# The experts' down weights, issued by ScalarE instead of the sync engine

## What is computed

```python
# t: 544 tokens x 1024; w_gate, w_up: 32 experts x 1024 x 256; w_down: 32 x 256 x 1024
expert_id = g_idx[:, None] * EXPERTS_PER_GROUP + top_i      # two experts for each token
gates = jnp.einsum('tk,tke->te', wts, jax.nn.one_hot(expert_id, N_EXPERTS, dtype=f32))
hg = jnp.einsum('td,edf->tef', t, w_gate)
hu = jnp.einsum('td,edf->tef', t, w_up)
hid = jax.nn.silu(hg) * hu * gates[:, :, None].astype(hg.dtype)
out = jnp.einsum('tef,efd->td', hid, w_down)
```

## Time and profile before

| | us |
|---|---|
| median of 3 executions | 1947.9 |
| lowest, highest | 1943.09, 2301.11 |
| the profiled execution, its own time | 1946.74 |
| its span in the trace | 1944.8 |

### The profile page before, as it was taken

The page is one execution under the profiler, slowest core; times in us unless marked ns, Lnnn a source line. Parts: engine busy times, 40 slices in busy tenths (PEclk is TensorE's granted clock), DMA queues, the critical chain, the costliest instruction groups (busy, mean ns, idle before and its releaser), DMA issues. The chain is left out here.

```text
span 1944.8 us, 25289 instructions
## 1 busy us (share of the span) xinstructions
PE 1489.6 (77%) x10126; PEld 1071.9 (55%) x10126; DVE 682.2 (35%) x1255; ACT 460.2 (24%) x799; POOL 212.6 (11%) x320
## 2 busy tenths in 40 slices
PE   3699789945499977799669888825996949988852
PEld 0699644421199943399445544415996935544421
DVE  2422255541224456563431111144244361111106
ACT  1322255521113352331301100123223220110012
POOL 2000023210000033200011100020002001100010
PEclk7799899877699887789879999957998969999985
DMA  7122496559522240321669999840222187999952
GB/s 266 30 88 78 152 369 244 216 191 365 187 65 87 72 174 1 141 87 44 270 241 392 390 389 400 309 136 24 86 88 67 51 366 282 384 395 396 393 215 90
DMA packets 133584, 399.59 MB, mean 205 GB/s; under 512 B 15842, under 2 KB 67682, under 8 KB 110690
## 3 DMA queue, kind: packets, MB, share of 16 engines
q1 hardware_dynamic: 114370, 359.01, 49.1%
q10 hardware_dynamic: 11488, 21.24, 3.0%
q0 software_dynamic: 7616, 17.84, 2.9%
HBM read 368.72 MB, written 37.19 MB: 209 GB/s over the span
## 5 line engine op out<-in xcount | busy, mean ns | idle before, releaser
L2647 PE MATMUL ex_gups<-ex_gu,ex_he 128*64 128x256 f32 x2048 | 257.7, 409 | 57.4 <-DMA ex_gu<-in_moe_w_up 54.5
L2647 PEld LDWEIGHTS ex_gups<-ex_gu,ex_he 128*64 128x64 f32 x2048 | 153.3, 147 | 143.2 <-DMA ex_gu<-in_moe_w_up 61.0
L2692 DVE TENSOR_TENSOR ex_hid<-ex_sg,ex_gups 128x128 f32<-128x128 f32 x64 | 18.4, 288 | 313.4 <-ACT ex_sg L2716 313.4
L225 PE MATMUL sc_ps<-h_hi,sc_hi 128*128 128x272 f32 x384 | 111.8, 291 | 20.6 <-PEq L2168 20.6
L2665 PE MATMUL ex_yps<-ex_dn,ex_hid_t 128*64 128x512 f32 x512 | 123.9, 604 | 0.9 <-issue 0.9
L2625 POOL DMA_INDIRECT ex_hg<-h_rows,route_tok x64 | 60.2, 941 | 529.1 <-PE ex_trps L2637 418.9
L225 PE MATMUL sc_ps<-h_hi,sc_w_r 128*128 128x272 f32 x384 | 112.2, 292 | 0.0
L225 PE MATMUL sc_ps<-hT_r,sc_hi 128*128 128x272 f32 x384 | 111.4, 290 | 0.0
L225 PE MATMUL xbcz_ps<-mixT_r,xbcz_hi 128*128 128x272 f32 x320 | 93.4, 292 | 16.6 <-DVE xbcz_w_r L322 16.6
L225 PE MATMUL xbcz_ps<-mixT_r,xbcz_w_r 128*128 128x272 f32 x320 | 93.6, 293 | 0.0
L225 PE MATMUL xbcz_ps<-hT_r,xbcz_hi 128*128 128x272 f32 x320 | 93.1, 291 | 0.0
(11 more groups left out here) (468 smaller groups left out, 3191.3 us busy)
## 6 DMA issues: line engine op xcount, KB each, us to landing
ex_gu<-in_moe_w_gate SPq DMA_DIRECT2D x64, 1024.0 KB
ex_gu<-in_moe_w_up SPq DMA_DIRECT2D x64, 1024.0 KB
ex_dn<-in_moe_w_down SPq DMA_DIRECT2D x64, 1024.0 KB
ada_rest_w<-in_ada_w SPq DMA_DIRECT2D x40, 1024.0 KB, 6.5
as_pages<-in_cache_kT SPq DMA_DIRECT2D x32, 512.0 KB, 6.2
as_pages<-in_cache_v SPq DMA_DIRECT2D x32, 512.0 KB, 5.2
y_rows<-ex_yo ACTq DMA_DIRECT2D x128, 128.0 KB
qkv_w<-in_mix_w_in SPq DMA_DIRECT2D x12, 1024.0 KB, 5.3
```

What stands on the lines that cost most here:

```text
L225: last = nc.tensor.matmul(ps[:, h, 0:HALF], w[:, j, f], x(j)[:, cols], start=(j == 0 and n == 0), stop=(j == kt - 1 and n == 2))
L2647: last = nc.tensor.matmul(gu_ps[64 * q:64 * q + 64, :, :], he[n % 2][:, j, :], ex.gu[n % S][:, :, j, q * P:(q + 1) * P], start=(j == 0), s ...
L2692: nc.vector.tensor_tensor(hid[:, :], sg[:, :], gu_ps[:, 1, :], ALU.mult).then_inc(done["hid"], 1)
```

## The change

The sync engine no longer waits for the down product and no longer loads down weights in the main pass. ScalarE issues the load of the down weights of expert `n + 5` in `keep_result(n)`, after its wait for the down product of `n`, before the wait for the earlier result's transfers and before the copy. Its condition is the same: the product that last read this buffer is done. The loads ahead (experts 0 to 4) and the second pass stay as they are.

```diff
@@ sync_main
                 b = n % S
                 sp.wait_ge(done["gu"], n - S + 1)
                 ex.load_gu(sp, b, n, ex.gu_ready[b])
-                sp.wait_ge(done["y"], n - S + 1)
-                ex.load_dn(sp, b, n, ex.dn_ready[b])
 
@@ scalar_main
             def keep_result(n):
                 p = n % 2
                 act.wait_ge(done["y"], n + 1)
+                if n + S < NE:
+                    ex.load_dn(act, n % S, n + S, ex.dn_ready[n % S])
                 if n >= 2:
                     act.wait_ge(put[p], 32 * (n // 2))
                 nc.scalar.activation(yo[p][:, :], y_ps[p][:, :], ACT.Copy).then_inc(done["yo"], 1)
```

## The result

The changed kernel takes 1970.0 us in the median of 4 executions (1959.4 to 1971.5), the one before 1945.5. The execution of before at 2301 us was disturbed: it is in the 1945.5, but not in the ratio. The ratio is 1.013, 95% interval 1.007 to 1.019: slower by 1.3%, which is under the 2% that such a measurement can tell, but outside its interval. Run once more, beside 16 executions of before, it took 1964.0 us, ratio 1.0125 (1.0099 to 1.0151). The profiled execution took 1969.7 us (span 1967.9), 23.1 us of span more than before.

A forecast was written before the change was run, and what follows sets the result against it. Experts' phase: TensorE sets the pace first, transfers from about the thirteenth expert (9.2 us each). Per layer +17.4 us at the end less 6.1 gives +11.3; 22 for both layers on 1946.7 makes 1969 us, range 1947 to 1984.

The forecast's parts named there:

- the right case: Experts' phase: ScalarE's copy is held by earlier writes and a backlog is worked off at the end; 1960 to 1984, chance 0.62.
- The gap at the start: Start of each layer's experts: 2.5 us of idle transfers while the sync engine waits for a down product; filled by the change.
- Turns packet by packet: The two hardware queues alternate packets whatever their size, so ScalarE's queue needs 11.9 us per expert while the sync queue is full.
- The guard: Copy L2706 of expert n waits for the write of n-2; closes at about expert 2 or 3, growing up to 4.8 us an expert.
- TensorE's first long stop: First layer's experts: TensorE first stands long at expert 5 to 7, some 1040 to 1055 us, not at 1087.
- The settled part: Middle of the experts' phase: the period is again the sum of the transfers, 9.2 us, with nothing lost per expert.
- The end: End of each layer's experts: 23 us left after loads against 5.6, net +11.3 us first layer, +9 to +11 second.
- the idle time before L2706: Sign at ScalarE's copy, first layer: idle time rises from 92.4 to some 250 us and ends with the write.
- up to 3.9: Result writes in ScalarE's queue: issue and receipt take up to 3.9 us, from a shortest landing of 4.6 us.
- the first rival: ScalarE's queue keeps up, the copy is never held by writes; +2.4 us a layer, 1951 to 1952, chance 0.22.
- The second: Rival: ScalarE's queue runs dry while TensorE is held, period over 9.2 us; +20 a layer on top, 2009, chance 0.10.
- The third: Rival, not slower: down loads come last without the copy being held by writes; 2.5 + 3.7 us less a layer, 1934, chance 0.06.

The follow-up runs named there:

- the sync engine's order: Kernel before, all weights still on the sync engine's queue, but gate and up of n issued ahead of down of n-1: 1931.6 us, ratio 0.9940.
- its control: Kernel before, with only the results' transfers issued by GpSimd instead of ScalarE and down loads unmoved: 1953.1 us, ratio 1.0060.

## Why the prediction was right

It said 1969 us in a range of 1947 to 1984, and the measured median is 1970.0. That they agree to 1 us is luck: the change cost 24.5 us in the medians and not 22, before came out at 1945.5 and not 1946.7, and run again the changed kernel took 1964.0. The larger chance went to the right case, and its steps held as follows.

**The gap at the start.** It is filled: gate and up of expert 6 left right after the product of expert 1, and the first stop of TensorE came from elsewhere. The run with the sync engine's order shows what freeing gate and up is worth, 4 to 6 us a layer, of which the gap is 2.5.

**Turns packet by packet.** 80 to 83 packets in the same 2 us, with loads in both queues, and 75 to 75 with 8 KB pieces in both. Six buffers with 8 KB pieces against six alone (11 and 14 us less a stretch), and the same pieces in one queue (1.7 and 0.5), show that the number of packets in ScalarE's queue matters, and little their size as such.

**The guard.** I put its first closing at expert 2 or 3; it is expert 3 (1026.94 to 1030.29). TensorE's first long stop, forecast for 1040 to 1055, is at 1041.

**The settled part.** The DMA engines stay at 1.01 to 1.02 and the rate at 387 to 397 GB/s, as before; gate and up land 13.1 us after their issue and lie ready. Nothing is lost per expert. But it is less even than I had it: from 1051.68 to 1223.52 us the sync engine's loads of gate and up go out 9.0 us apart in the mean, in steps of 7.1 to 15.2 and not every 9.2. TensorE does some experts at its own pace and then stands.

**The end.** Forecast: 23 us left after the loads, loads 6 us sooner, +11.3 in the first layer, +9 to +11 in the second. Measured: 24 left, loads 3 to 4 us sooner (251 against 254), +13.7 and +8.0; again, 27, 6, +14.9 and +9.1. The sums, 21.7 and 24.0, enclose the 22, with the first layer above its 11.3 and the second at or below its range. The term that was off in the first execution is the time of the loads' end, by 2 to 3 us, which is little more than it can be read to. In the second execution that term was right, and what was left was 27 for 23: from the issue of the last down load (1237.13) to the end of the stretch it took 32.7 us, as forecast (32; 30.6 in the first execution), but the load was through after some 6 us and not 8 to 9. A part of the first is seen: near the end, with hardly anything but ScalarE's queue, the DMA engines are not full. The windows row of 1236 to 1244 us:

```profile
1236.00:1244.00 8.00, 6.59 (x47) 4.04 (x45) 1.09 (x3) 1.47 (x3) 0.93 (x1) 1.00 0.86 321
```

A share of 0.86 over 8 us is 1.1 us lost. The rest I can't place.

**What was wrong in detail.** I wrote that the idle time before L2706 would rise to some 250 us; it is 184.0. I had added 6 to 7 us of stall for each of 22 experts to the 92.4 of before, but a copy that waits for a write no longer waits for its product: the two do not add. The 159.0 us put down to the write are what I had multiplied out.

I also misread. They are of the whole tensor `y_rows`, and the trace of before gives no landing time for the results' transfers: the 4.6 to 15.3 us are those of the zeros written to it earlier and of the reads by `phase_combine`. Where a trace has the figure (the sync engine's order, whose writes are free of loads as before), a result lands 2.3 us after its issue at the least and 7.0 in the median. So the "up to 3.9" for issue and receipt was too much, 1.6 at most, and the argument from 5.7 us for the first rival had no ground. The guard's first closing was forecast at expert 2 or 3, and the later of the two came; the sum does not use the term.

And the account was incomplete in one place: it knew one limit of ScalarE's queue and there are two. That a long queue holds the issuing engine stood in the sync engine's rows (2.36 us in the earlier trace rows), and I priced it only for one down load, not for the two writes, which took up to 11.17 us once the guard was gone. In the changed kernel the guard closes first, so the sum did not suffer; the forecasts of the experiments did.

**The rivals.** The first (the new queue keeps up, 1951) is not what happened, but it is nearly what the run with GpSimd's writes shows once its control is taken off: 2 us of stretches where the rival has 5, with gate and up awaited to the end. The second (starved engines) did not occur: no stretch of the settled part is under 1.01. The third had the end right that I thought impossible, down weights last and little left after them: it is the run with six buffers and 8 KB pieces, at 1928 for my 1934. The changed kernel did not reach it.

## What to carry to other kernels

Before moving loads to an engine that also writes results, look at what that engine waits for from its own queue: here a copy waited for a write that now stood behind a 1 MB load, and in the rows before the change that wait was not visible at all. While both queues had work, they got equal numbers of packets (105 to 104, 80 to 83, 75 to 75) and not equal bytes; count packets to tell a queue's pace beside another one. In a phase that is bound by transfers, a change that leaves the DMA engines full can still cost time, by what lies loaded and unused when the last load lands; the time left after the last load, 6 us before and 24 after, is the row to read. The gain was to be had without the second queue: keep one queue and put into it first what is needed first (257 us a stretch in place of 261 to 263).

## What the hardware showed that I had not expected

- With a long queue even the issue of a small transfer can hold the engine: 11.17 us for two transfers of 128 KB, 1.12 us with a short queue.
- With results issued by GpSimd the next phase began some 6 us later than with those issued by ScalarE (24 against 18 us from the last down product to the first transpose of the combine), in two kernels alike. It is not the transfers: in the control the last two land 2.4 us after their issue, and from 1258 us on there are next to no packets. The first gather of the combine comes 10.7 us after the end of GpSimd's last issue; before, 4.8 us after the end of ScalarE's. What fills that time the runs don't show.
- With ScalarE's queue nearly alone at the end of a stretch, the DMA engines stood at 0.86 from 1236 to 1244 us, while in the settled part they stay at 1.01. It is no limit of one queue: from 1244 to 1246 us q10 alone reaches 96.1%. Before the change the last loads run out slowly. These runs don't show the reason for either.
